# A two-layer hybrid backbone: load orders and load sizes at the starts of four kinds of stage

## The reference

```python
h = rmsnorm(x, norm_g) * (1 + scale) + shift          # scale, shift, gate from silu(c) @ w_mod + b_mod
s = split_cols(h @ w_in)                              # 18 named segments of columns
y = concat([mlstm(s), diff_attn(s), ssd(s), hgrn2(s)])  # 256 columns each
x = x + gate * (y @ w_out)
...
return rmsnorm(x, final_g)                            # after the last layer
```

## Time and profile before

| | us |
|---|---|
| median of three runs | 5933.59 |
| lowest, highest | 5918.35, 5942.54 |
| the profiled execution | 5931.59 |
| its span (first to last instruction) | 5929.7 |
| TensorE busy in the span | 5450.2 (92%) |
| VectorE, ScalarE, GpSimd busy | 2914.2, 1675.7, 2308.2 |

### The profile page before, as it was taken

How to read it: one execution, slowest core, us unless ns; L and a number is a source line. 1 busy time by engine, 2 the same in 40 slices (tenths; PEclk the granted TensorE clock), 3 DMA queues, 4 the chain that set the end, 5 groups by cost and what they waited for, 6 DMA issues and landing times. The chain is left out here.

```text
span 5929.7 us, 74508 instructions
## 1 busy us (share of the span) xinstructions
PE 5450.2 (92%) x26120; PEld 2867.8 (48%) x26120; DVE 2914.2 (49%) x4926; ACT 1675.7 (28%) x4031; POOL 2308.2 (39%) x1695
## 2 busy tenths in 40 slices
PE   5999999967888799998999999999688879999989
PEld 2445454436777433332445544544467763333334
DVE  1444545434777655551113455455557766555212
ACT  1111111111444244444002212212123333444411
POOL 0112211113444279998001111111234435999910
PEclk7999999986999899999999999999779988999989
DMA  6232322247222100000623333332462220000032
GB/s 237 88 103 97 103 99 99 96 159 225 83 95 97 64 1 8 8 6 7 245 104 109 103 99 103 99 101 93 140 192 92 85 79 24 5 4 8 5 126 87
DMA packets 380770, 530.62 MB, mean 89 GB/s; under 512 B 109073, under 2 KB 266569, under 8 KB 374065
## 3 DMA queue, kind: packets, MB, share of 16 engines
q1 hardware_dynamic: 354690, 453.12, 23.1%
q10 hardware_dynamic: 19728, 40.41, 1.8%
q0 software_dynamic: 6048, 33.11, 1.5%
HBM read 372.13 MB, written 154.08 MB: 89 GB/s over the span
## 5 line engine op out<-in xcount | busy, mean ns | idle before, releaser
L607 PE MATMUL psum<-group_W,projection_hT 128*128 128x512 f32 (+4 forms) x5016 | 1954.9, 547 | 5.9 <-DVE projection_hT L729 5.7
L607 PEld LDWEIGHTS psum<-group_W,projection_hT 128*128 128x128 f32 x5016 | 951.2, 191 | 973.5 <-issue 932.0
L2266 POOL TENSOR_TENSOR attention_PS<-attention_PS 128x1024 f32<-128x1024 f32 x548 | 1265.8, 2351 | 83.6 <-ACT attention_PS L2399 75.9
L2312 DVE TENSOR_REDUCE attention_mxp<-psum 128x1 f32<-128x512 f32 (+1 forms) x1016 | 654.5, 686 | 543.4 <-PE psum L2448 543.4
L459 POOL TENSOR_TENSOR projection_cx<-projection_cx,projection_cw 128x768 f32<-128x768 f32 x102 | 186.8, 1831 | 1688.5 <-DMA projection_cw<-in_ss_conv_w 1688.5
L2399 ACT ACTIVATE attention_PS<-psum 128x512 f32<-128x512 f32 (+1 forms) x1168 | 630.6, 592 | 719.4 <-PE psum L2502 701.5
L2448 PE MATMUL psum<-attention_QK 32*128 32x512 f32 (+1 forms) x2592 | 772.6, 612 | 9.1 <-DVE attention_mxp L2301 6.1
L2496 PE MATMUL psum<-attention_QK 32*128 32x512 f32 x2336 | 665.6, 643 | 0.0
L2514 PE MATMUL psum<-attention_PS,attention_va 128*64 128x512 f32 x2336 | 628.9, 617 | 0.0
L680 ACT ACTIVATE projection_ut<-psum 128x256 f32<-128x256 f32 (+2 forms) x322 | 127.3, 406 | 1417.9 <-PE psum L607 1406.7
L2632 PE MATMUL psum<-output_W,output_yT 128*128 128x512 f32 x1088 | 478.5, 599 | 21.1 <-DMA output_W<-in_w_out 21.1
(11 more groups left out here) (361 smaller groups left out, 6151.5 us busy)
## 6 DMA issues: line engine op xcount, KB each, us to landing
u<-projection_ut SPq DMA_DIRECT2D x240, 256.0 KB, 2.0
projection_cx<-xbc SPq DMA_DIRECT2D x306, 128.0 KB, 2.2
projection_cw<-in_ss_conv_w SPq DMA_DIRECT2D x102, 384.0 KB, 4.4
mixing_hg<-u SPq DMA_DIRECT2D x34, 1024.0 KB, 5.1
group_W<-in_w_in SPq DMA_DIRECT2D x8, 2316.0 KB, 18.8
output_y<-y SPq DMA_DIRECT2D x34, 512.0 KB, 4.5
group_W<-in_w_in POOLq DMA_DIRECT2D x6, 2316.0 KB, 28.7
xbc<-projection_ut SPq DMA_DIRECT2D x34, 384.0 KB, 2.4
```

Of the source, the lines that this page charges most:

```text
L607: ins = nc.tensor.matmul(ps[n % RING][:, lo - c0:lo - c0 + w], hT[b][:, q], W[q][:, lo:lo + w], start=(q == 0), stop=(q == KT - 1))
L2266: G.tensor_tensor(SA[x % 2][:, rs, 0:w], one[:, rs, 0:w], PT[i % PTB][:, rs, 0:w], ALU.add) \
L2312: bk.release(V.tensor_reduce(mxp[x % 2][:, q:q + nn, 2 * pr + j, a], bk[job, j][:, 0:nn * (hi - lo)].rearrange("p (q n) -> p q n", q=nn), ...
```

## The change

Four stages are touched, and one buffer is added.

In **gates**, `pair` is loaded ahead of `brow` and the six `wm` blocks instead of behind them.

In **states**, the seven loads of a step become five: `fi` comes in one load (for the backward direction its two halves lie side by side in `u` and are one run of 512 columns), and `key` and the values come in one load of 512 columns into a new tile `kv`. ScalarE copies the values from `kv` into `va` at the start of its step (`spread`), TensorE's increments wait for `spread`, and so does SPq before it reuses a buffer.

For **attention**, tiles 0 to 5 of the query and key columns (1.5 MB) are loaded into the new buffer `k.ahead` at the end of the states' loads, and the transposes of these tiles read from there. The first of attention's four loads is gone.

In **output**, each of the eight blocks of `W` has a semaphore. For tile 0, TensorE does both halves of block q as soon as that block is in, and transposes tile 1 behind all of them instead of between the halves. GpSimd still waits for all eight.

```diff
--- before.py
+++ after.py
@@ -924,11 +924,11 @@
                 for o, i in ((tri[:], k.x["c_tri"]), (pick[:], k.x["c_pick"])):
                     sp.dma_start(o, i).then_inc(s["tables_in"], 16)
                 if more:
+                    sp.dma_start(pair[:], k.x["c_pair"]).then_inc(s["bias_in"], 16)
                     sp.dma_start(brow[:], k.x["b_mod"][l + 1].unsqueeze(0)).then_inc(s["bias_in"], 16)
                     wl = k.x["w_mod"][l + 1].rearrange("(k p) n -> p k n", p=P)
                     for n in more:
                         sp.dma_start(wm[n][:], wl[:, :, n * 512:(n + 1) * 512]).then_inc(s[f"wm_in{n}"], 16)
-                    sp.dma_start(pair[:], k.x["c_pair"]).then_inc(s["bias_in"], 16)
                 sp.wait_ge(s["out_ready"], 1)
                 sp.dma_start(k.gt.rearrange("t p n -> p t n"), GT[:]).then_inc(s["stored"], 16)
                 sp.wait_ge(s["rows_ready"], 3)
@@ -1215,9 +1215,10 @@
     ahead = CT if l == DEPTH - 1 else 0
     BACK = [(1, t) for t in (*range(CT - 1, -1, -1), *range(NT - 1, CT - 1, -1))]
     TILES = [(0, t) for t in range(ahead)] + BACK
-    IN, RING, NLOAD = 4, 4, 7
+    IN, RING, NLOAD = 4, 4, 5
+    ALONG = CT + QG
     with ExitStack() as c:
-        key = [k.sb(c, f"key{b}", [P, 256]) for b in range(IN)]
+        kv = [k.sb(c, f"kv{b}", [P, 512]) for b in range(IN)]
         va = [k.sb(c, f"va{b}", [P, H, 65]) for b in range(IN)]
         fi = [k.sb(c, f"fi{b}", [P, 512]) for b in range(IN)]
         kk = [k.sb(c, f"kk{b}", [P, 256]) for b in range(IN)]
@@ -1232,7 +1233,7 @@
         zeros = k.sb(c, "zeros", [P, STW])
         ones = k.sb(c, "ones", [P, 1])
         tri = k.sb(c, "tri", [P, 4, P])
-        s = k.sems(c, "consts_in memsets exps_done weighted keyed updated "
+        s = k.sems(c, "consts_in memsets spread exps_done weighted keyed updated "
                       + " ".join(f"in{b}" for b in range(IN)) + " " + " ".join(f"st_stored{b}" for b in range(RING)))
         steps = range(ahead + NT - 1)
         last = len(steps)
@@ -1252,18 +1253,21 @@
                     b, (d, t) = n % IN, TILES[n]
                     u = k.u[t]
                     if n >= IN:
+                        sp.wait_ge(s["spread"], n - IN + 1)
                         bk.wait(sp, ("ml_hg", n - IN))
                         bk.wait(sp, ("ss", n - IN))
                         sp.wait_ge(s["weighted"], n - IN + 1)
                         sp.wait_ge(s["updated"], n - IN + 1)
-                    for o, i in ((fi[b][:, 0:256], u[:, OFF["hg_f"] + d * 256:OFF["hg_f"] + d * 256 + 256]),
-                                 (fi[b][:, 256:512], u[:, OFF["hg_i"]:OFF["hg_i"] + 256]),
+                    f = OFF["hg_f"]
+                    rows = u[:, f + 256:f + 768] if d else u[:, f:f + 1024].rearrange("p (a n) -> p a n", a=2)[:, :, 0:256]
+                    for o, i in ((fi[b][:] if d else fi[b][:].rearrange("p (a n) -> p a n", a=2), rows),
+                                 (kv[b][:], u[:, 256:768]),
                                  (gt[b][:], k.gt[t]),
-                                 (key[b][:], u[:, 256:512]),
                                  (xb[b][:], k.xc[t, :, 0:512]),
-                                 (kk[b][:], u[:, OFF["hg_k"] + d * 256:OFF["hg_k"] + d * 256 + 256]),
-                                 (va[b][:, :, 0:64], u[:, 512:768].rearrange("p (h w) -> p h w", h=H))):
+                                 (kk[b][:], u[:, OFF["hg_k"] + d * 256:OFF["hg_k"] + d * 256 + 256])):
                         sp.dma_start(o, i).then_inc(s[f"in{b}"], 16)
+                sp.dma_start(k.ahead[:], k.u[0:ALONG, :, OFF["da_q"]:OFF["da_q"] + 512].rearrange("t p n -> p t n")) \
+                    .then_inc(k.ahead_in, 16)
 
             @block.gpsimd
             def _(gp):
@@ -1279,7 +1283,7 @@
                     if n >= 2:
                         bk.wait(gp, ("ml_hg", n - 2))
                         bk.wait(gp, ("ss", n - 2))
-                    nc.gpsimd.tensor_tensor(h4(kp[n % 2][:]), h4(key[b][:]), g("wk"), ALU.mult)
+                    nc.gpsimd.tensor_tensor(h4(kp[n % 2][:]), h4(kv[b][:, 0:256]), g("wk"), ALU.mult)
                     nc.gpsimd.tensor_tensor(h4(xw[n % 2][:]), h4(xb[b][:, 0:256]), g("ws"), ALU.mult) \
                         .then_inc(s["weighted"], 1)
 
@@ -1347,6 +1351,10 @@
 
                 act.wait_ge(s["memsets"], 1)
                 for n in steps:
+                    loaded(act, n)
+                    if n >= IN:
+                        bk.wait(act, ("ml_hg", n - IN))
+                    nc.scalar.activation(va[n % IN][:, :, 0:64], h4(kv[n % IN][:, 256:512]), ACT.Copy).then_inc(s["spread"], 1)
                     bk.wait(act, ("sum", n))
                     if n >= 2:
                         act.wait_ge(s["keyed"], n - 1)
@@ -1378,6 +1386,7 @@
 
                 def increments(n):
                     pe.wait_ge(s["weighted"], n + 1)
+                    pe.wait_ge(s["spread"], n + 1)
                     pe.wait_ge(s["keyed"], n + 1)
                     bk.take(pe, ("ml_hg", n))
                     b = bk[("ml_hg", n)]
@@ -2170,7 +2179,7 @@
         idb = k.sb(c, "idb", [P, P], BF16)
         oneb = k.sb(c, "oneb", [P, P], BF16)
         ones = k.sb(c, "ones", [P, DQ])
-        s = k.sems(c, "consts_in memsets x_in0 x_in1 x_in2 x_in3 v_in key_mm key_copied pro_mm pro_read "
+        s = k.sems(c, "consts_in memsets x_in1 x_in2 x_in3 v_in key_mm key_copied pro_mm pro_read "
                       "dve_step act_step pool_step lam_dot lam_exp ready mneg_ready mm_ready pv_done added acc_free sq_ready "
                       "ssq_ready rstd_ready out_ready z_in0 z_in1 stored0 stored1")
         bk = Turns(k, c, uses)
@@ -2183,6 +2192,8 @@
                                    k.x["da_lambda"][l].rearrange("a n -> (a n)").unsqueeze(0).to_broadcast([P, 4 * DQ]))):
                     sp.dma_start(out_, in_).then_inc(s["consts_in"], 16)
                 for n, (lo, hi) in enumerate(parts):
+                    if n == 0:
+                        continue
                     sp.dma_start(xb[:, lo:hi], k.u[lo:hi, :, OFF["da_q"]:OFF["da_q"] + 512].rearrange("t p n -> p t n")) \
                         .then_inc(s[f"x_in{n}"], 16)
                 for t in range(NT):
@@ -2431,11 +2442,12 @@
                     for t in tiles:
                         for n, (lo, hi) in enumerate(parts):
                             if t == lo:
-                                pe.wait_ge(s[f"x_in{n}"], 16)
+                                pe.wait_ge(s[f"x_in{n}"] if n else k.ahead_in, 16 if n else 16 * (l + 1))
                         if t >= 2:
                             pe.wait_ge(s["key_copied"], t - 1)
                         for a in range(4):
-                            ins = nc.tensor.transpose(k.bank[4 + t % 2][:, a * P:(a + 1) * P], xb[:, t, a * P:(a + 1) * P], k.ident[:])
+                            ins = nc.tensor.transpose(k.bank[4 + t % 2][:, a * P:(a + 1) * P], (xb if t >= CT + QG else k.ahead)[:, t, a * P:(a + 1) * P],
+                                                      k.ident[:])
                         ins.then_inc(s["key_mm"], 1)
 
                 rows = lambda r: slice(DQ * r, DQ * r + DQ)
@@ -2578,7 +2590,7 @@
         eps = k.sb(c, "eps", [P, 1])
         sm = many("sm", 2, [P, 4])
         junk = k.sb(c, "junk", [P, D])
-        s = k.sems(c, "w_in gate_in y_in0 y_in1 y_in2 x_in0 x_in1 x_in2 scaled summed normed final stored0 stored1 act_step memsets")
+        s = k.sems(c, " ".join(f"w_in{q}" for q in range(KT)) + " gate_in y_in0 y_in1 y_in2 x_in0 x_in1 x_in2 scaled summed normed final stored0 stored1 act_step memsets")
         bk = Turns(k, c, uses)
         xc_, xl = layer_input(k, l)
 
@@ -2599,7 +2611,7 @@
 
                 load(0)
                 for q in range(KT):
-                    sp.dma_start(W[:, q], wv[:, q]).then_inc(s["w_in"], 16)
+                    sp.dma_start(W[:, q], wv[:, q]).then_inc(s[f"w_in{q}"], 16)
                 load(1)
                 for a in range(2):
                     sp.dma_start(gate[:, a], k.modrow[l, a, 2 * D:3 * D].unsqueeze(0).to_broadcast([P, D])) \
@@ -2611,7 +2623,8 @@
             @block.gpsimd
             def _(gp):
                 gp.memset(eps[:], EPS).then_inc(s["memsets"], 1)
-                gp.wait_ge(s["w_in"], 16 * KT)
+                for q in range(KT):
+                    gp.wait_ge(s[f"w_in{q}"], 16)
                 for q in range(len(k.W)):
                     gp.dma_start(k.W[q][:], k.x["w_in"][l + 1, q * P:(q + 1) * P]).then_inc(k.w_early, 16)
 
@@ -2634,8 +2647,17 @@
                     bk.done(ins, ("o", n, a))
 
                 turn(0)
-                pe.wait_ge(s["w_in"], 16 * KT)
-                for n in range(N):
+                for a in range(2):
+                    bk.freed(pe, ("t", 0, a))
+                for q in range(KT):
+                    pe.wait_ge(s[f"w_in{q}"], 16)
+                    for a in range(2):
```

(9 more changed lines are left out.)

## The result

The changed kernel takes 5880.43 us, the median of four runs (5875.27 to 5892.71). The kernel before, run on the same chip, takes 5930.78 us. The ratio is 0.9919, with a 95% interval of 0.9900 to 0.9938, so 50 us are gone. The forecast was 5876. The profiled execution of the changed kernel is its longest one (5892.71 us, span 5891.0), and against the profiled one of before it is only 38.7 us of span shorter.

What follows compares the result with a forecast made beforehand. TensorE was busy for 92% of the span, so only its waits could be won. Gates 20.5, states 16, attention 9.6, output 1 and 8.4 sum to 55.5 us: from 5931.6 to 5876 us, range 5851 to 5898.

Steps and rivals of the forecast that it cites:

- 20.5 with ends 16 and 25: Gates, layer 0: us gained when TensorE no longer waits for `pair`, with lower and upper end.
- The clock of the four blocks: Gates, layer 0: four more `wm` blocks could each meet the other clock, 2.2 us apiece.
- the chain moves forward as a whole: Gates, layer 0: everything behind the transposes of `M` stays the same and shifts earlier; 20.5 us taken.
- whether longer runs lift the rate: States: 2 KB runs were taken to raise 284 GB/s towards 387; 16 us gained, only 2 if not.
- the one from the rate to the period: States: loads at 387 GB/s need 3.2 us, under TensorE's 3.77, so periods fall to 3.85 us.
- rival (a): States stay bound by bytes, leaving 2 of 16 us: 5890 us; chance 0.20.
- The copy on ScalarE: States: the added copy, 36 in all, costed at nothing under the sums; 22 us without that cover.
- Rival (b): States: TensorE rises to the full clock, loads set 3.2 us, 22 us more gained: 5854 us; chance 0.10.
- 9.6 with ends 7 and 10.2: Attention, both layers: us gained by loading the first tiles ahead, 4.8 a layer, with lower and upper end.
- the next in line: Attention start: ScalarE's exponential still holds its first copy, which moves 5.1 us earlier in layer 0, not the whole wait.
- a hole of 4.6 us for `y` of tile 2: Output, layer 0: TensorE waits for this late load; with 3.2 us of low clock, about 1 us net gain remains.
- Rival (c): Output, layer 0: low clock lasts many tiles, 222 us if 16 run slow, 6098 us; chance 0.02.

Runs made afterwards that it cites:

- g_busy: Changed kernel with 9, 2 and 12 dummy products in three holes of gates of layer 0; stage 59.1 us, run 5878.77 us.

## Why the forecast held, and where it did not

**Gates: right.** The term was 20.5 with ends 16 and 25; the nine profiles give 19.1. The start of the transposes moved by 19.9 us (46.8 to 26.9), where 20.1 to 21.2 had been worked out. The clock of the four blocks was rightly kept as an uncertainty: the same code took from 64.0 to 71.0 us. But the sentence that the chain moves forward as a whole hid something. With `pair` out of the way TensorE stands 2.76 us for VectorE's cast between two full-clock stretches, and the blocks behind it, which the earlier trace rows show at both clocks, ran at half. `g_busy`, with its three holes filled, shows that such waits are worth 5 to 12 us.

**States: wrong in size, and by the step on the loads.** The forecast said that the outcome hangs on whether longer runs lift the rate. The joined loads do, 305 to 361 GB/s at a full share. The step that failed is the one from the rate to the period, 1.22 MB in 3.2 us, less than 3.77. It took the loads as a stream, but they are released by the update of four steps before. Issue and landing take about two periods (2.5 and 5.2 us), so the transfers cannot run ahead: the period stayed at 4.18 us at a DMA share of 0.93. 3.3 us came instead of 16, not clear of the profiles' spread: the outcome of rival (a), but not by its cause as stated, since at a full share the bytes bind only when the ring is deep. The copy on ScalarE cost nothing with four buffers, as forecast (0.42 us, in the shadow of the sums). Rival (b), the full clock, is real too; it appears in stretches with six buffers.

**Attention: right in mechanism, and a little beyond its range.** 9.6 with ends 7 and 10.2; measured 10.9, and 4.5 and 4.2 us to the first reduction. Each stage differs by some 3 us from one profile to the next, most of it before the maxima of the prologue are ready, and the term had no room for that. ScalarE's exponential was the next in line, as said.

**Output 0: right in mechanism.** Forecast a hole of 4.6 us for `y` of tile 2 and 3.2 us of low clock; the rows show 3.40 and 1.2 in the 32 passes (0.6 more in the transposes). The term was 1 (0 to 4) and 2.7 was measured. Its own numbers, 3.8 less 3.2, gave 0.6. Rival (c), slowness over many tiles, did not happen: the next turn is at its pace again.

**Output 1: right.** 8.4 forecast, 8.4 measured.

**The sum.** Of 55.5 us, 13 are missing in states and 1.4 in gates, and attention and output 0 gave 3 more: the five terms came to 44 us. The total, 5880 against 5876, is closer than its terms, and that is luck. The stages that nobody touched, and what the profiles and the runs differ by, brought 7 us that the forecast did not have.

## What to carry to other kernels

For a stage fed by a ring of buffers, count how long before its use a load is issued, and compare that with issue time plus landing time; only when this fits does the rate of the transfers mean anything for the period, and bigger transfers and a deeper ring were worth more together than one by one. When a wait goes, read the next one in every queue behind it: a copy on ScalarE stood behind copies that were not ready, a load of 0.5 MB landed beside 14 MB of another queue, and in both cases reordering took the wait out. A short wait between full-clock stretches of TensorE can cost more afterwards than it lasts, and independent products put into three of them paid for themselves (59.1 us for the stage instead of 64.0 to 71.0).
